# Mixture-of-experts layer, one core: a pair's product transposes and down-projection moved from behind the pair's extra blocks into the first of them

## What is computed

```
def expert_group(args):
    tok, wt, e = args
    xb = h_pad[tok]
    hid = jax.nn.silu(xb @ w1[e]) * (xb @ w3[e])
    return (hid @ w2[e]) * wt[:, None]
```

## Time and profile before

| what | value |
| --- | --- |
| median of 3 runs | 1351.01 us (1348.84 to 1366.55) |
| the profiled execution's own time | 1354.66 us |
| its span, first to last instruction | 1352.0 us |
| experts on TensorE, first up-projection to the last pair's down-projection | 661.5 to 1297.4 us |
| matmuls, busy in the whole span | 1039.3 us (77%) |
| mean granted clock of TensorE | 0.923 |

### The profile page before, as it was taken

The page is one execution under the profiler, slowest core; times in us unless marked ns, Lnnn a source line. Parts: engine busy times, 40 slices in busy tenths (PEclk is TensorE's granted clock), DMA queues, the critical chain, the costliest instruction groups (busy, mean ns, idle before and its releaser), DMA issues.

```text
span 1352.0 us, 23540 instructions
## 1 busy us (share of the span) xinstructions
PE 1039.3 (77%) x8381; PEld 658.7 (49%) x8382; DVE 429.4 (32%) x807; ACT 236.7 (18%) x474; POOL 217.8 (16%) x361
## 2 busy tenths in 40 slices
PE   3289999997678399997376887778786788856865
PEld 2287877875467244454243544435443354423432
DVE  4323232334964212577421111111111111111118
ACT  1122122333545300021000111011110111000110
POOL 0001120200000000110222222223221222321211
PEclk9999999998779799989688889999998898988988
DMA  8665867552017296137587789987999988899955
GB/s 297 141 228 201 286 209 265 188 187 94 0 59 247 72 339 213 61 124 312 164 292 292 272 322 409 394 315 286 402 385 393 340 296 295 303 391 405 415 214 237
DMA packets 98651, 349.67 MB, mean 259 GB/s; under 512 B 15141, under 2 KB 20453, under 8 KB 73886
## 3 DMA queue, kind: packets, MB, share of 16 engines
q1 hardware_dynamic: 83006, 315.56, 63.3%
q0 software_dynamic: 13856, 30.13, 6.8%
q10 hardware_dynamic: 1728, 3.15, 0.6%
HBM read 331.25 MB, written 29.59 MB: 267 GB/s over the span
## 4 chain that ended last, share of the span: by engine, by line
PE 26%; DMA 16%; issue 6%; DVE 2%; SPq 1%; ACT 0%; POOL 0%; POOLq 0%; DVEq 0%; ACTq 0%
PE PS L1719 8%; DMA hT<-h_rows,ixo 8%; DMA W<-w 7%; PE PS L1734 6%; PE PS L1750 4%; PE PS L1775 4%; PE PS L1789 2%; PE PS L1725 1%; DMA vec<-ln_b 1%; PE PS L1707 1%; PE PS L1765 1%; DVE hid L1836 0%; PE PS L1742 0%; DMA W<-expert_rows 0%; DVE oaT L1871 0%
## 5 line engine op out<-in xcount | busy, mean ns | idle before, releaser
L1719 PE MATMUL PS<-W,XT 128*32 128x256 f32 x2048 | 130.2, 411 | 52.1 <-DMA W<-w 28.4
L1734 PE MATMUL PS<-W,XTo 128*64 128x256 f32 x1216 | 141.2, 385 | 0.0
L1719 PEld LDWEIGHTS PS<-W,XT 128*32 128x32 f32 x2048 | 80.0, 118 | 120.3 <-issue 95.8
L1734 PEld LDWEIGHTS PS<-W,XTo 128*64 128x64 f32 x1216 | 94.4, 139 | 44.4 <-issue 11.2
L428 DVE TENSOR_TENSOR w_lo<-raw,w_hi 128x2048 fp32r<-128x2048 f32 x26 | 59.5, 2290 | 145.8 <-ACT w_hi L390 145.8
L1750 PE MATMUL PS<-W,hidTo 128*64 128x512 f32 x304 | 88.4, 706 | 16.3 <-DVE hidTo L1844 10.8
L361 PE MATMUL PS<-w_hi,u_hi 128*128 128x512 f32 x240 | 95.5, 398 | 0.1
L361 PE MATMUL PS<-w_hi,u_lo 128*128 128x512 f32 x240 | 94.8, 395 | 0.0
L361 PE MATMUL PS<-w_lo,u_hi 128*128 128x512 f32 x240 | 94.7, 395 | 0.0
L1775 PE MATMUL PS<-W,hidT 128*32 128x512 f32 x512 | 70.4, 666 | 27.3 <-issue 24.9
L390 ACT CAST w_hi<-raw 128x2048 fp32r<-128x2048 f32 x26 | 49.5, 1905 | 138.1 <-DMA raw<-w_in 106.7
(11 more groups left out here) (333 smaller groups left out, 1506.8 us busy)
## 6 DMA issues: line engine op xcount, KB each, us to landing
W<-w SPq DMA_DIRECT2D x192, 1024.0 KB, 13.3
raw<-w_in SPq DMA_DIRECT2D x26, 1024.0 KB, 9.5
oaT<-w_ada SPq DMA_DIRECT2D x8, 1536.0 KB, 7.8
W<-expert_rows SPq DMA_DIRECT2D x24, 512.0 KB, 12.6
obT<-w_ada SPq DMA_DIRECT2D x8, 512.0 KB, 8.0
kc<-cache_k_diff SPq DMA_DIRECT2D x8, 512.0 KB, 4.7
vc<-cache_v_diff SPq DMA_DIRECT2D x8, 512.0 KB, 3.5
Wa<-p_a SPq DMA_DIRECT2D x4, 1024.0 KB, 9.7
```

The lines of the kernel that those rows point to most:

```text
L1719: mm = pe.matmul(PS[64 * h + 32 * c:64 * h + 32 * c + 32, UP_B + i, 0:F], XT[:, i, k, 32 * c:32 * c + 32], t.W13[:, 2 * i + c, h, k], star ...
L1734: mm = pe.matmul(PS[64 * h:64 * h + 64, XH_B, 0:F], XTo[:, k], t.W13[:, slot, h, k], start=k == 0, stop=k == KD - 1)
```

## The change

On TensorE, a pair with at least one extra block goes through a new order, `lead`, in its first extra block: up-projection of the extra block, transposes of the pair's product, transposes of the next extra block's rows, transposes of the extra block's product, down-projection of the pair, down-projection of the extra block. Its other extra blocks run in the loop as before, and behind the last of them nothing is left to do. A pair with no extra block keeps the old order. VectorE gets the matching order. The transposed products of extra blocks get their own half of the PSUM bank. SP loads a slot's W2 when the pair's down-projection and the slot's last extra down-projection (`o_y`) are both done; before, the order on TensorE alone ensured the second. The calls are the same; the code for them is written once more for each slot, as `lead` stands in two branches, and three extra-block loops stand where there were two.

```
 sp:
                     sp.wait_ge(yy_mm, n + 1)
-                    stand_alone(sp)
                     for c in range(2):
+                        sp.wait_ge(o_y, before[c] + 1)
+                        stand_alone(sp)
                         load_down(sp, t, expert_at(it + 1, 2 * i + c), 2 * i + c)
 pe:
+                def lead(slot, g):
+                    extra_up(slot, g)
+                    turn_hid(n, i)
+                    extra_turn(g)
+                    extra_hid(g)
+                    down(n, i, it)
+                    extra_down(slot, it, g)
+
+                with pe.If(first[0] < first[2]):
+                    with pe.If(first[0] < first[1]):
+                        lead(2 * i, first[0])
+                        extra(pe, first[0] + 1, first[1], extra_block(2 * i, it))
+                        extra(pe, first[1], first[2], extra_block(2 * i + 1, it))
+                    with pe.If(first[0] >= first[1]):
+                        lead(2 * i + 1, first[1])
+                        extra(pe, first[1] + 1, first[2], extra_block(2 * i + 1, it))
+                with pe.If(first[0] >= first[2]):
+                    turn_hid(n, i)
+                    down(n, i, it)
 dve:
-                dve.tensor_copy(hidTo[...], PS[:, HT_B, 0:P]).then_inc(o_he, 1)
+                dve.tensor_copy(hidTo[...], PS[:, HT_B, P:2 * P]).then_inc(o_he, 1)
...
+                def lead(g):
+                    turned_hid(n, i)
+                    product(g)
+                    turned_product(g)
+                    rows_of(n, i, it)
+                    extra_rows(g)
```

More of the change, by code:

```diff
@@ L1608, in body @@
                     sp.wait_ge(h_mm, n + 1)
+                    before = []
                     for c in range(2):
                         used = sp.value_load(t.ov[0:1, bass.ds(n * 2 + (c + 1), 1)], min_val=0, max_val=XB)
+                        before.append(used)
                         sp.wait_ge(o_h, used + 1)
@@ L1726, in turn_extra, with extra_up, extra_turn @@
                 mm.then_inc(o_xt, 1)
+            def extra_up(slot, g):
+                pe.wait_ge(o_xe, g + 1)
+                stand_alone(pe)
+                for k in range(KD):
+                    for h in range(2):
+                        mm = pe.matmul(PS[64 * h:64 * h + 64, XH_B, 0:F], XTo[:, k], t.W13[:, slot, h, k], start=k == 0, stop=k == KD - 1)
+                mm.then_inc(o_h, 1)
+            def extra_turn(g):
+                pe.wait_ge(o_in, (g + 2) * 16)
+                stand_alone(pe)
+                turn_extra()
@@ new lines, in extra_hid, with extra_down @@
+            def extra_hid(g):
+                pe.wait_ge(o_hid, g + 1)
+                stand_alone(pe)
+                for j in range(2):
+                    mm = pe.transpose(PS[:, HT_B, P + SLOTS * j:P + SLOTS * j + SLOTS], hido[:, P * j:P * j + P], t.ident[0:SLOTS, 0:SLOTS])
+                mm.then_inc(o_ht, 1)
+            def extra_down(slot, it, g):
+                pe.wait_ge(t.wdown_in[slot], (it + 1) * 16)
+                pe.wait_ge(o_he, g + 1)
+                pe.wait_ge(o_ye, g + 1)
+                stand_alone(pe)
+                for j in range(2):
+                    for h in range(2):
+                        mm = pe.matmul(PS[64 * h:64 * h + 64, XY_B], hidTo[:, j], t.W2[:, slot, j, CW * h:CW * h + CW], start=j == 0, stop=j == 1)
+                mm.then_inc(o_y, 1)
@@ L1728, in extra_block @@
             def extra_block(slot, it):
                 def step(g):
[L1730 to L1751, removed]
-                return step
[L1754 to L1760, removed]
+                    extra_up(slot, g)
@@ L1761, in body, with turn_hid @@
+                    extra_turn(g)
+                    extra_hid(g)
+                    extra_down(slot, it, g)
+                return step
+            def turn_hid(n, i):
                 pe.wait_ge(hid_done, n + 1)
@@ L1766, in body, with down @@
                 mm.then_inc(ht_mm, 1)
+            def down(n, i, it):
                 for c in range(2):
@@ L1777, in body @@
                 mm.then_inc(yy_mm, 1)
+            def body(n, i, it, fixed):
+                first = extra_bounds(pe, n)
+                up(n, i, it)
+                if within(fixed, 1):
+                    turn(n + 1, (i + 1) % PW, it + (i + 1) // PW)
+                def lead(slot, g):
+                    extra_up(slot, g)
+                    turn_hid(n, i)
+                    extra_turn(g)
+                    extra_hid(g)
+                    down(n, i, it)
+                    extra_down(slot, it, g)
+                with pe.If(first[0] < first[2]):
[9 more added lines that the diff above has]
+                    down(n, i, it)
             pe.sem_inc(o_h, 1)
+            pe.sem_inc(o_y, 1)
             turn(0, 0, 0)
@@ L1837, in hidden, with product @@
                                   PS[SLOTS:P, UP_B + i, 0:F].rearrange("r (p j) -> r p j", j=2), ALU.mult).then_inc(hid_done, 1)
-            def step(g):
+            def product(g):
                 dve.wait_ge(o_silu, g + 1)
@@ L1842, in step, with turned_product, extra_rows, turned_hid @@
                                   PS[SLOTS:P, XH_B, 0:F].rearrange("r (p j) -> r p j", j=2), ALU.mult).then_inc(o_hid, 1)
+            def turned_product(g):
                 dve.wait_ge(o_ht, g + 1)
-                dve.tensor_copy(hidTo[:, :, :].rearrange("p j s -> p (j s)"), PS[:, HT_B, 0:P]).then_inc(o_he, 1)
+                dve.tensor_copy(hidTo[:, :, :].rearrange("p j s -> p (j s)"), PS[:, HT_B, P:2 * P]).then_inc(o_he, 1)
+            def extra_rows(g):
                 dve.wait_ge(o_out, g * 16 + 16)
-                dve.wait_ge(o_y, g + 1)
+                dve.wait_ge(o_y, g + 2)
                 dve.tensor_copy(Yo[:, :], PS[:, XY_B]).then_inc(o_ye, 1)
+            def step(g):
+                product(g)
+                turned_product(g)
+                extra_rows(g)
+            def turned_hid(n, i):
+                dve.wait_ge(ht_mm, n + 1)
+                once_above(dve, yy_mm, n - PW + 1)
+                dve.tensor_copy(hidT[:, i].rearrange("p j s -> p (j s)"), PS[:, HT_B, 0:P]).then_inc(ht_ev, 1)
+            def rows_of(n, i, it):
+                dve.wait_ge(yy_mm, n + 1)
+                once_above(dve, y_out[i], it * 16)
+                dve.tensor_copy(Y[:, i], PS[:, Y_B]).then_inc(yy_ev, 1)
             def body(n, i, it, fixed):
@@ L1851, in body @@
                 hidden(n, i)
[L1852 to L1859, removed]
+                def lead(g):
+                    turned_hid(n, i)
+                    product(g)
+                    turned_product(g)
+                    rows_of(n, i, it)
+                    extra_rows(g)
+                with dve.If(first[0] < first[2]):
+                    lead(first[0])
+                    extra(dve, first[0] + 1, first[2], step)
+                with dve.If(first[0] >= first[2]):
+                    turned_hid(n, i)
+                    rows_of(n, i, it)
             dve.sem_inc(o_ye, 1)
```

## The result

The changed kernel takes 1422.86 us (median of 4, 1420.28 to 1423.81), the kernel before in the same series 1349.92 us. The ratio is 1.049, 95% interval 1.045 to 1.0535: 73 us slower, where 20 us faster were forecast. Rival 1 came about: the code no longer fits.

A forecast was written before the change was run, and what follows sets the result against it. TensorE mostly sets the pace, in places the weight stream. Of 46 us gained on TensorE, 20 were kept after the stream, first passage and end: 1334.7 us profiled, 1331 median, range 1314 to 1358.

The forecast's parts named there:

- Rival 1: TensorE's loop no longer fits instruction memory and is fetched each turn: 1381 us, range 1360 to 1425, chance 0.17.
- the fit of the loop: TensorE's loop grows from 3.4 to 6.6 packets and would still fit 8 blocks; no fetch cost in the sum.
- the first passage through the code: Pairs 0 to 3, longer code run first: 0 to 2.9 us each, 1 taken, 4 us off.
- the prices of a pair: TensorE's gain per pair: 2.0 us with one extra block, 2.3 us with more.
- From the extra transposes to the next pair: TensorE, pair with one extra block: 4.4 us to the next up-projection, instead of 6.57.
- The VectorE copy that goes ahead: VectorE copy now preceding the extra block's product: delays it by up to 0.29 us, 0.2 taken.
- Waits for weights: Sign in TensorE's waits: weights up from 28.4 to 40 or 50 us, gathered rows from 27.9 to about 10.
- above 0.9: Sign by stretch: DMA share above 0.9 where it was 0.76 to 0.83.
- the full stretch at the end: Pairs 24 to 31, weight queue full: nothing added, 3 us of the gain taken off.
- Rivals 2: The weight stream takes nearly all the gain, empty queue being load latency: 1349 us, chance 0.10.
- rival 3: More gain kept, through the clock and W2 given back some 3 us earlier: 1321 us, at least 1305, chance 0.15.
- clock term: TensorE's granted clock: shorter waits for gathered rows might avoid slow matmuls, giving 5 to 15 us.

The follow-up runs named there:

- the unused code: The changed kernel with only the lead for slot 0, plus a never-taken branch over 130 transposes in each body: 1597.13 us.
- the kernel with slot 0 alone: The changed kernel with one of its two leads dropped, keeping the one for a first extra block in slot 0: 1335.56 us, again 1337.4 us.
- Half the unused code: The changed kernel with only the lead for slot 0, plus a never-taken branch over 60 transposes in each body: 1359.15 us.

## Why the prediction was wrong

**The step that failed** is the fit of the loop. The sum puts fetches inside the loop at nothing; the only place where they stand is rival 1, with 0.17 and "Against it: nothing but the sum of blocks". The runs showed 62 us for them in its place. A second term of the sum, the first passage through the code, was 4 us and came to some 24. The length was right (6.6 blocks counted, 6.6 foreseen). What was not weighed is that a loop of 6.6 blocks lies across 8 of them at most starts and across 7 at only about a third of them (starts 0 to 0.36 behind a border). By the rule above 8 is one more than stay, so the fit was the exception and not the likely case. The Trainium skill (Runtime: NRT & Kernel Launch, Instruction fetch mechanics) gives 2048 instructions, 8 blocks, refilled in order; the runs agree if one of the eight is held for the block ahead. They don't agree with its sentence on two lines, if that is read for TensorE too: loops of 3.4 to 5.9 blocks stay with 1 to 3 packets in 487 us.

**The price of rival 1.** 1381 us were given, 1360 to 1425 as its own range, and 1423 lies just within. By difference of runs the fetches inside the loop cost 1422.9 - 1360.7 = 62 us (the changed kernel against itself at another start), where 50 stood in the text. That the sizes are so close is partly luck: the 2.9 us a body were read from a single stall in the first turn, and 26 times that came to 75 us, a third of it taken off; measured are nine stalls with no releaser of 4.4 to 14.3 us between 745 and 1282 us, 77 us together, and turns without any between them. By packets of the whole loop it is 1.3 us each in the changed kernel (62 / 46) and 2.0 in the unused code (220 / 109).

**First passage.** The term was 4 us, from 1 a pair in pairs 0 to 3, with nothing for the pairs behind the loop. It is 1360.7 - 1336.5 = 24 us between the changed kernel at its good start and the kernel with slot 0 alone (mean of its two series; 21 to 26 us by the ratios), although the first has six more pairs in the new order. Half the unused code, which changes nothing in the order, cost the same 24 us. By the starts of the pairs, against the second series of slot 0 alone, some 9 us are lost from pair 0 to pair 6 and some 12 more between pair 27 and pair 31. At start 0.45 the last pairs lose more, 22 us instead of 13 between pairs 27 and 31 against the first series; most of what parts 1373.2 from 1360.7 lies there. TensorE in the changed kernel at start 0.60, pair 3 and pair 29 (L1741 is its extra block's up-projection):

```profile
741.61 6.42 PE L1727 MATMUL PS<-W,XT 128*32 128x256 f32 x64 [8.31 <-issue]
...
1248.14 5.75 PE L1727 MATMUL PS<-W,XT 128*32 128x256 f32 x64 [11.38 <-issue]
...
1259.45 5.24 PE L1741 MATMUL PS<-W,XTo 128*64 128x256 f32 x32 [4.92 <-issue]
```

**The order itself.** Here the working held, as far as it was tested. The kernel with slot 0 alone has the new order in 15 of 21 pairs and hardly a fetch in its loop. By its starts of pairs the gain over before is 16, 13, 26 and 24 us at pairs 13, 18, 24 and 31, and 20 us at the end of the last down-projection; 2 us of each are there at pair 0, where the change has done nothing yet. That leaves 14, 11, 24, 22 and 18. The second series gives 15, 10, 24, 22 and 19 in the same way; the prediction said 14, 12, 24, 21 and 20, for all 21 pairs and with 4 us off for the first passage. At the prediction's prices the six new pairs before pair 13 are worth 5 x 2.3 + 2.0 = 13.5 us, with nothing off, and 14 and 15 were measured. So the prices of a pair hold, and the total of 20 us meets partly by luck: 1334.75 us in the first profiled execution against 1334.7 summed, but 1342.85 in the second, and six pairs fewer. Pair 16 of it, the same pair as in the earlier trace rows:

```profile
983.94 3.67 PE L1736 MATMUL PS<-W,XTo 128*64 128x256 f32 x32
...
988.99 0.30 PE L1748 MATMUL PS<-ident,hido 64*128 64x64 f32 x2 [0.60 <-DVE hido L1875]
989.25 1.92 PE L1786 MATMUL PS<-W,hidT 128*32 128x512 f32 x16
991.10 1.94 PE L1758 MATMUL PS<-W,hidTo 128*64 128x512 f32 x8
993.54 3.66 PE L1722 MATMUL PS<-W,XT 128*32 128x256 f32 x64 [0.51 <-DMA W<-w]
```

From the extra transposes to the next pair are 4.55 us, 4.4 were said, and the last of it is a wait for weights. The VectorE copy that goes ahead moved the extra product by 0.04 us (0.60 instead of 0.56), not by 0.2. TensorE's waits in this kernel, 680 to 1350 us:

```profile
PE PS L1722 <- DMA W<-w: 41.5, 8, 11.6
PE PS L1722 <- issue: 24.3, 20, 2.6
PE PS L1728 <- DMA hT<-h_rows,ixo: 15.7, 11, 3.2
```

Waits for weights of 40 to 50 us and for gathered rows of about 10 were to be seen; 41.5 and 15.7 are. And by stretch (bounds moved with the pairs):

```profile
661.00:775.00 114.00, 87.15 (x823) 48.14 (x812) 30.26 (x60) 11.94 (x25) 28.89 (x46) 0.91 0.79 287
...
1039.00:1154.00 115.00, 97.30 (x942) 53.87 (x930) 23.80 (x45) 14.46 (x30) 35.59 (x61) 0.97 0.90 330
1154.00:1259.00 105.00, 72.79 (x781) 39.70 (x781) 15.10 (x29) 9.64 (x20) 21.17 (x35) 0.90 1.01 405
```

The share rose from 0.76 to 0.79 and from 0.83 to 0.90, so "above 0.9" came about in neither, and the full stretch at the end (1.01) took back 2 of the 26 us by pair 31, where 3 were said. One reading of the earlier trace rows was off: from the transposes of pair 31's product to its scatter the trace before has 1294.18 to 1298.97, 4.79 us and not 4.94; the sum doesn't use it.

**Rivals 2 and 3** are not borne out by the kernel with slot 0 alone: the stream did not take the gain (14 to 15 us by pair 13), and the 1321 us of rival 3 were not reached. Its clock term doesn't show (granted clock 0.909 to 0.935 in the four executions, 0.905 to 0.930 before), and of W2 given back earlier nothing shows either.

The balance of the 73 us: 62 for fetches in the loop and 24 for code passed once (less what the new order gives in six more pairs), less 13 for the order in 15 pairs (1349.9 - 1336.5). That the three close is how they were formed. In its own two series the order is worth 18 to 22 us (ratios 0.987 and 0.984 of 1350), so 5 to 9 us of the balance are uncertain.

**Open** is why the same code costs 220 us at start 0.16 and 90 at 0.91 (107 packets behind pair 3 against 46), and which blocks a turn fetches. Open is also why the borders lie a third of a block away from the count, and so whether the good starts are the same in a program with something else ahead of it. That 7 blocks stay and one is held for the block ahead is inferred from which starts are fast; no run shows a block by itself. The rule also rests on one length beyond 5.9 blocks; none between was tried. A version in which the pairs behind the loop cost no fetches was not tried either.

## What to carry to other kernels

Count the instructions of a looped part, branches not taken included, and ask across how many blocks of 256 it lies. Here up to 5.9 blocks stayed, and at 6.6 blocks a change that adds code lost more than it gained in order or didn't, by where the loop happened to start and by which of its branches were entered. Two checks are quick: packets on the instruction queue inside the loop, and waits with no releaser that are longer than the usual ones (2.6 us at most in front of an up-projection before the change). Write the special case only for the side that occurs most: here one lead for slot 0 took 15 of the 21 pairs at 576 instructions a body, where two took all of them at 841, and the shorter one was faster by 24 us even against the good start of the longer.

## What the hardware showed

- 90 instructions that no execution reaches, ahead of a loop, made the same kernel 220 us faster (1597.1 to 1377.2), and 68 made another 50 us faster (1422.9 to 1373.2).
- A loop of 6.6 blocks of 256 TensorE instructions brings 3 to 6 packets between 745 and 1232 us at starts of 0.45, 0.52 and 0.60 of a block, and 37 to 76 at 0.12 to 0.18 and 0.91 to 0.93. Loops of 3.4 to 5.9 blocks bring 1 to 3.
- In the changed kernel no packet comes in pairs 4 to 8, 12 to 14 and 18; the bursts begin with pairs 9, 15 and 19 (4, 4 and 5 packets), which are pairs of the second body with extra blocks.
- The stalls before an up-projection that come with these fetches last up to 14.3 us, and matmuls behind them run slower: the up-projection behind the 11.07 us gap took 6.25 us instead of 3.66. The granted clock of the stretch 940 to 1056 us is 0.85, 0.91 before.
